# Decay rows of a chunked scan: repeated over the partitions by TensorE into PSUM instead of by a DRAM round trip

## The reference, cut to what matters

```python
cs = jnp.cumsum(dtc * a.reshape(G, R), axis=2)
seg = cs[:, :, :, None] - cs[:, :, None, :]
decay = jnp.where(tril, jnp.exp(jnp.where(tril, seg, 0.0)), 0.0)
cb = jnp.einsum('bcign,bcjgn->bcijg', cc, bc)
y_diag = jnp.einsum('bcijgr,bcjgrp->bcigrp', decay * cb[..., None], xdt)
...
y_off = jnp.einsum('bcign,bcgrpn,bcigr->bcigrp', cc, h_prev, jnp.exp(cs))
```

## Time and profile before

| what | value |
|---|---|
| median of three executions | 1598.22 us |
| the profiled execution | 1598.22 us |
| its span, first to last instruction | 1596.5 us |
| mean granted TensorE clock | 0.984 of full |
| busy share of the span: PE, DVE, ACT, POOL | 97%, 18%, 13%, 8% |
| mean DMA rate | 249 GB/s |

### The profile page before, as it was taken

How to read it: one execution, slowest core, us unless ns; L and a number is a source line. 1 busy time by engine, 2 the same in 40 slices (tenths; PEclk the granted TensorE clock), 3 DMA queues, 4 the chain that set the end, 5 groups by cost and what they waited for, 6 DMA issues and landing times.

```text
span 1596.5 us, 44448 instructions
## 1 busy us (share of the span) xinstructions
PE 1548.9 (97%) x20574; PEld 1305.1 (82%) x20574; DVE 284.1 (18%) x680; ACT 204.8 (13%) x527; POOL 131.4 (8%) x200
## 2 busy tenths in 40 slices
PE   7999999999999999998999999999999999999998
PEld 5667666666666667666999999999999999999897
DVE  2455520000000245553100000000000000000021
ACT  1245310000000034521000000000000000000000
POOL 4311125000000020111100000000000000000100
PEclk9999999999999999999899999999999999999999
DMA  9933429976323432332899999999999999999991
GB/s 250 269 114 89 128 82 273 334 246 218 119 93 113 112 112 67 100 117 93 280 355 343 358 359 352 357 346 339 369 349 355 356 346 359 344 365 360 348 354 36
DMA packets 199228, 397.39 MB, mean 249 GB/s; under 512 B 13723, under 2 KB 69667, under 8 KB 198889
## 3 DMA queue, kind: packets, MB, share of 16 engines
q1 hardware_dynamic: 180664, 346.26, 63.4%
q0 software_dynamic: 16816, 45.42, 9.4%
q10 hardware_dynamic: 1568, 2.91, 0.6%
HBM read 359.87 MB, written 36.63 MB: 248 GB/s over the span
## 4 chain that ended last, share of the span: by engine, by line
PE 95%; DVE 2%; issue 1%; ACT 1%; DMA 1%; SPq 0%; DVEq 0%; ACTq 0%
PE bank L1298 33%; PE bank L1320 16%; PE bank L1210 13%; PE bank L755 7%; PE bank L1227 6%; PE bank L1051 2%; PE bank L738 2%; PE bank L1068 2%; PE bank L724 1%; PE bank L1035 1%; PE bank L1024 1%; PE bank L1260 1%; PE bank L678 1%; PE bank L709 1%; PE bank L1041 1%
## 5 line engine op out<-in xcount | busy, mean ns | idle before, releaser
L1298 PE MATMUL bank<-arena,ring 128*64 128x108 f32 x11264 | 532.9, 257 | 9.6 <-issue 8.7
L1298 PEld LDWEIGHTS bank<-arena,ring 128*64 128x64 f32 x11264 | 526.8, 138 | 15.5 <-issue 13.1
L1320 PE MATMUL bank<-arena,ring 128*64 128x108 f32 x5632 | 263.2, 256 | 0.2
L1320 PEld LDWEIGHTS bank<-arena,ring 128*64 128x64 f32 x5632 | 261.7, 137 | 0.8 <-issue 0.6
L1210 PE MATMUL bank<-hnT,ring 128*128 128x336 f32 x704 | 200.8, 449 | 1.8 <-DVE hnT L1676 1.8
L1210 PEld LDWEIGHTS bank<-hnT,ring 128*128 128x128 f32 x704 | 134.6, 191 | 68.1 <-issue 3.2
L755 PE MATMUL bank<-hnT,ring 128*128 128x336 f32 x384 | 119.8, 457 | 0.0
L2133 DVE TENSOR_TENSOR arena<-arena,bank 128x432 f32<-128x432 f32 (+1 forms) x48 | 27.2, 567 | 509.3 <-PE bank L1298 509.3
L1227 PE MATMUL bank<-arena,ring 128*128 128x336 f32 x352 | 99.6, 446 | 0.0
L755 PEld LDWEIGHTS bank<-hnT,ring 128*128 128x128 f32 x384 | 70.5, 192 | 34.7 <-issue 6.4
L1227 PEld LDWEIGHTS bank<-arena,ring 128*128 128x128 f32 x352 | 66.9, 190 | 32.6
(11 more groups left out here) (360 smaller groups left out, 1079.1 us busy)
## 6 DMA issues: line engine op xcount, KB each, us to landing
ring<-in_moe_w_gate SPq DMA_DIRECT2D x88, 1024.0 KB, 6.2
ring<-in_moe_w_up SPq DMA_DIRECT2D x88, 1024.0 KB, 6.3
ring<-in_moe_w_down SPq DMA_DIRECT2D x88, 1024.0 KB, 5.9
ring<-in_w_in SPq DMA_DIRECT2D x16, 1024.0 KB, 6.7
ring<-in_w_gate SPq DMA_DIRECT2D x11, 1024.0 KB, 20.6
ring<-in_w_up SPq DMA_DIRECT2D x11, 1024.0 KB, 18.5
xg_rows<-arena POOLq DMA_DIRECT2D x1, 10800.0 KB, 71.8
y_rows<-arena POOLq DMA_DIRECT2D x1, 10800.0 KB, 112.8
```

The costliest lines, as they stand in the source:

```text
L1298: ins = mm(into[rows, SLOTS * fi:SLOTS * fi + SLOTS], weights[:, c, col:col + 64], xg[:, k0 + c, :], start=(k0 + c == 0 and fi == 0), stop ...
L1320: ins = mm(bank[5 + c // 4][rows, SLOTS * (c % 4):SLOTS * (c % 4) + SLOTS], weights[:, col:col + 64], hid[:, f, :], start=(f == 0 and c % ...
```

## The change

`csrow` no longer goes to DRAM. A new PE step `row_decays(pr)` multiplies, for each of the pair's two heads, a [8, 128] stationary tile (column h of the identity, repeated over 128 columns) with `csrow`, [8, 336]. The product puts the head's row on all 128 partitions of PSUM bank 3 or 4. ACT's `decays` reads that bank and waits for `seg_psum`. A bank is written again when `decay_exp` says that ACT has read it. `sample_states` uses bank 0 alone, and waits for DVE to have read its previous half. The stationary and moving operands need 8 partitions.

```diff
-        head_sums_kept = nc.dram_tensor("head_sums_kept", [LAYERS, HEADS, NT], F32, kind="Internal").ap()
...
-        decay = [take(544), take(512)] + [qk_[:, i * PCOLS:(i + 1) * PCOLS] for i in range(2)]
-        decay_rows = qk_[:, 2 * PCOLS:2 * PCOLS + 2 * NT]
+        decay = [take(544), take(512)] + [qk_[:, i * 512:(i + 1) * 512] for i in range(2)]
...
-        def sstate_bank(pr, q):
-
-            return 3 if q and pr < 3 else 0
...
+                def row_decays(pr):
+
+                    for h in (2 * pr, 2 * pr + 1):
+                        if h >= 2:
+                            pe.wait_ge(decay_exp, 8 * l + h - 1)
+                        mm(bank[3 + h % 2][:, 0:NT], ident[0:8, h:h + 1].to_broadcast([8, 128]), csrow, start=True, stop=True).then_inc(seg_psum, 1)
+
...
-                    if pr:
-                        pe.wait_ge(sstate_ready, 2 * n + (1 if pr == 3 and q else q - 1))
-                    mm(bank[sstate_bank(pr, q)][:, :], xw[pr % 2][0:80, 2, :], Bexp[0:80, 4 * q:4 * q + 4, :], start=True, stop=True).then_inc(sstate_psum, 1)
+                    if pr or q:
+                        pe.wait_ge(sstate_ready, 2 * n + q)
+                    mm(bank[0][:, :], xw[pr % 2][0:80, 2, :], Bexp[0:80, 4 * q:4 * q + 4, :], start=True, stop=True).then_inc(sstate_psum, 1)
...
                 sample_attend(1)
+                row_decays(0)
...
                 states_turned(0)
+                row_decays(1)
                 pe.wait_ge(mixsq_ready, 3 * l + 1)
...
                 for pr in range(4):
+                    if pr in (1, 2):
+                        row_decays(pr + 1)
                     if pr < 3:
                         states_turned(pr + 1)
...
                     if pr == 3:
+                        pe.wait_ge(decay_exp, 8 * (l + 1))
                         attention_part(4, 3)
...
-                def decay_rows_wanted(pr):
-                    act.wait_ge(sums_kept, 16 * (l + 1))
-                    if pr:
-                        act.wait_ge(decay_exp, 8 * l + 2 * pr)
-                    act.dma_start(decay_rows, head_sums_kept[l, 2 * pr:2 * pr + 2].rearrange("h t -> (h t)").partition_broadcast(128)).then_inc(decay_rows_here, 16)
-
...
-                        act.dma_start(head_sums_kept[l], csrow).then_inc(sums_kept, 16)
...
-                        R, E = decay_rows[:, NT * hh:NT * hh + NT], decay[h % 4]
-                        act.wait_ge(decay_rows_here, 16 * (4 * l + pr + 1))
+                        R, E = bank[3 + hh], decay[h % 4]
+                        act.wait_ge(seg_psum, 8 * l + h + 1)
...
-                    v.tensor_tensor(h0_[pr][:, 512 * q:512 * q + 512], h0_[pr][:, 512 * q:512 * q + 512], bank[sstate_bank(pr, q)][:, :], ALU.add).then_inc(sstate_ready, 1)
+                    v.tensor_tensor(h0_[pr][:, 512 * q:512 * q + 512], h0_[pr][:, 512 * q:512 * q + 512], bank[0][:, :], ALU.add).then_inc(sstate_ready, 1)
```

More of the change, by code:

```diff
@@ L405, in hymba_step @@
             sem(x) for x in ("s_probT_psum", "s_probT_dve", "s_probT_act", "s_att_psum"))
-        cb_psum, cb_ready, sums_kept, decay_rows_here, decay_exp, M_ready, ypair_psum, y_ready, Bexp_ready = (
-            sem(x) for x in ("cb_psum", "cb_ready", "sums_kept", "decay_rows_here", "decay_exp", "M_ready", "ypair_psum", "y_ready", "Bexp_ready"))
+        cb_psum, cb_ready, seg_psum, decay_exp, M_ready, ypair_psum, y_ready, Bexp_ready = (
+            sem(x) for x in ("cb_psum", "cb_ready", "seg_psum", "decay_exp", "M_ready", "ypair_psum", "y_ready", "Bexp_ready"))
         h0T_psum, h0T_act, h0T_dve, xw_ready, pstate_ready, sstate_psum, sstate_ready, half_psum, half_added = (
@@ L1541, in _ @@
                         act.wait_ge(tail_cols_ready, l + 1)
-                        decay_rows_wanted(0)
                     if u == 21:
@@ L1588, in _ @@
                 act.wait_ge(att_mixed, 3 * (l + 1))
-                decay_rows_wanted(1)
                 f(att_squares, mixT[:, 4:8, 256:NT], ACT.Square).then_inc(mixsq_ready, 1)
@@ L1596, in _ @@
                 states_turned(1)
-                decay_rows_wanted(2)
                 decays(2)
                 states_turned(2)
-                decay_rows_wanted(3)
                 decays(3)
```

## The result

The changed kernel took 1603.14 us (median of 16 runs, 1592.22 to 1610.46). The kernel before, on the same chip, took 1592.58 us (median of 16, 1588.70 to 1600.17). The ratio is 1.0054, with an interval of 1.0036 to 1.0073: the change costs 0.54%, some 8.6 us, and the interval leaves 5.7 to 11.6 us. Most of it is a fixed price of the new matmuls. The clock adds nothing that shows over many runs: the middle of their mean clocks is 0.984 for both kernels.

The account below looks back on a forecast made before the run. PE was taken as the bound: 3.89 us in layer 0 and 3.21 in layer 1 made 7.1, added to 1598.2, less 3.3 for a clock fall that goes, forecast 1602.0 us; the range ran from 1595.9 to 1608.6.

Parts of the forecast that it names:

- rival 4: ACT's DMA waits were on the path: all 11.3 us go, 9.04 come, 1595.9 us; chance 0.10.
- pairs 1 and 2: row_decays(2) and (3) at these pairs' starts, where PE runs without a break: nothing covers them, +2.26 us a layer.
- the passage: Serial stretch leading to layer 0's loop, with row_decays(0) ahead of the token rows: nothing covers its two matmuls, +1.13 us.
- pair 0: Layer 0, row_decays(1) ahead of L1116: partly hidden in PE's wait, 0.56 us of delay, taken as 0.5.
- so I keep 0.565: Price in us of one new matmul on PE, from 336-column float32 matmuls in the chain; two make a step of 1.13.
- Layer 1's passage and pair 0: row_decays(0) shifts DVE against POOL's L588, while PE's idle 2.10 us hides row_decays(1): middle of two cases, +0.95 us.
- DVE first: Layer 1: DVE's L1908 starts before POOL's L588, POOL is held 0.5 us, L1920 ends about 0.65 us later.
- POOL first: Layer 1: POOL's L588 starts before DVE's L1908, which is held instead of L1920; L1920 ends 1.2 us later.
- bound of 9.04 for all exposed: Upper end for both layers in us: four steps a layer at 1.13, 4.52 a layer, none hidden.
- -3.26: Layer 1's first fall of PE's clock, behind the idle time before pair 0's outputs, likelier than not goes: 3.26 us saved.
- Rival 3: New fall of the clock in layer 0's serial passage or at another PE wait in layer 1: 1608.6 us; chance 0.20.
- rival 5: Something else sets the time, as in the earlier run of 1590.5 us: at or under 1592; chance 0.05.

Follow-up runs that it names:

- two row tiles: Kernel before with a second tile for the rows, each pair's DMA asked for a pair earlier, no new matmul: 1590.30 us, ratio 0.9988.
- two filled kernels: Idle full-size matmuls in PE's waits: six a layer in the kernel before (1584.52 us, ratio 0.9946), five in the changed kernel (1597.29 us, 1.0020).
- before, once more: Kernel before, no edit, profiled a second time: one execution, 1598.96 us.
- placed one by one: Changed kernel with 128-partition row matmuls, several heads' matmuls placed apart, meant for where PE waits for DVE: 1591.95 us, ratio 0.9991.

## Why the prediction was right and wrong

**Right.** PE is the bound, and what the change adds is PE's time in the chain: the kernel before with the matmuls alone has the same loss. ACT's waits for the DMA were off the path (rival 4 falls with the two row tiles: 0.9988). ACT's new waits cost nothing; no L1036 was released by late decays, though ACT waited 32.5 us for PE. Right too was what lies bare: pairs 1 and 2 and the passage in full, pair 0 in part.

**The step that failed first: "nothing in the rows says that fewer partitions make a matmul shorter, so I keep 0.565".** I asked only whether a low tile would be quicker. It is dearer, by its neighbours: 1.46 us a step instead of 1.13. Term by term, forecast and measured at full clock: the passage of layer 0 1.13 and 1.32; pair 0 0.5 and 0.74; pairs 1 and 2 together 2.26 and 2.93. Layer 0: 3.89 forecast, 5.0 measured. A row that hints at it was in the trace of before, the 0.47 us ahead of the weight loads at 131.15, and I read PE's rows and not those of its loads; it shows that a change of height is paid, though not how much.

**Layer 1's passage and pair 0** had 0.95, between 0.65 (DVE first) and 1.2 (POOL first). Measured: +1.32 in the passage (the changed kernel's own has a fall of the clock in it, so this is from the same step in others: 6.79 us against 5.47), and pair 0 from 7.34 to 6.64, -0.70: +0.62 in all, as much as the end for DVE first. Layer 0's pair 0 took 5.90 us before, so the meeting of POOL and DVE cost layer 1 1.44; now pair 0 takes 6.64 in both layers, and PE no longer pays for it. But in the changed kernel's profile POOL and DVE hardly met. The timeline of DVE and POOL in the changed kernel, against the earlier trace rows:

```profile
674.72 1.89 POOL L582 TENSOR_TENSOR arena<-arena,const 80x1024 f32<-80x1024 f32 x1
...
676.47 0.56 DVE L1903 TENSOR_TENSOR arena<-arena,small 128x384 f32<-128x384 f32 x1
...
677.88 0.67 DVE L1915 TENSOR_TENSOR arena<-arena 128x496 f32<-128x496 f32 x1
```

POOL's L582 ends at 676.61, while L1903 (before: L1908) has just begun, and L1915 (before: L1920, 2.11 us) has its 0.67; the passage was late by its own fall of the clock. With 64 partitions and no such fall the same instructions meet:

```profile
669.08 2.55 POOL L582 TENSOR_TENSOR arena<-arena,const 80x1024 f32<-80x1024 f32 x1
669.32 0.55 DVE L1903 TENSOR_TENSOR arena<-arena,small 128x384 f32<-128x384 f32 x1
...
670.74 1.42 DVE L1915 TENSOR_TENSOR arena<-arena 128x496 f32<-128x496 f32 x1
```

POOL's takes 2.55 us instead of 1.89 and DVE's L1915 1.42 instead of 0.67: first POOL is held through L1903, then DVE through POOL's rest, and pair 0 takes 6.65 us all the same. That is the case of DVE first as forecast. It is the rule that the prediction quoted from the Trainium skill ("SBUF — State Buffer", "SBUF: two separate sides") in its other case, with one difference: POOL's record starts 0.24 us before DVE's, and it is POOL that is lengthened by about L1903's time. The start of a record doesn't say who holds the port. With pairs 1 and 2 (2.93) layer 1 is 3.6, forecast 3.21.

The sum: 8.6 us, forecast 7.1, measured 8.6 over the runs and 8.9 between the two filled kernels. That is within the forecast's own bound of 9.04 for all exposed, but for another reason: at 1.46 a step that bound is 11.7, and 3.1 of it don't show: 1.4 are hidden in PE's waits at pair 0, 0.3 are saved in the passages (1.32 a step and not 1.46), and 1.4 are what layer 1's meeting no longer costs. The match of 8.6 with 8.6 is better than it deserves: the interval is 3 us wide to either side, and what the experts give back isn't in the sum.

**The step that failed second: the clock's term as a whole, "-3.26".** The fall that it speaks of did go. From pair 0's outputs of layer 1 to the next `sample_states`, 4.75 us at full clock, all three profiled executions with neither new matmuls nor filling show a fall, and none of the seven with the new matmuls does. What failed is that its price was booked as the change of the clock over the whole kernel, as if no other fall came in its place. The table has the profiled executions, in us. Its first column of numbers is the way from `states_turned(0)` to pair 0's outputs, at full clock 5.90 before, 6.64 with low tiles and some 6.3 with full ones; the other three go from a pair's outputs to the next `sample_states`, at full clock 4.75.

| kernel | layer 0, up to pair 0 | layer 0, pair 3 | layer 1, pair 0 | layer 1, pair 3 |
|---|---|---|---|---|
| before | 5.90 | 4.76 | 8.01 | 6.37 |
| before, once more | 5.91 | 8.01 | 9.07 | 8.01 |
| two row tiles | 5.90 | 4.75 | 6.36 | 4.75 |
| changed | 8.26 | 8.01 | 4.75 | 8.01 |
| before with the matmuls | 8.28 | 8.01 | 4.75 | 4.75 |
| 32 partitions | 8.28 | 8.01 | 4.75 | 6.18 |
| 64 partitions | 6.64 | 4.75 | 4.76 | 6.19 |
| 128 partitions | 6.25 | 6.28 | 4.75 | 8.01 |
| placed one by one | 6.37 | 4.75 | 4.75 | 4.75 |

The falls in the scans cost 4.9 and 11.2 us in the two profiles of before and 9.4 in that of the changed kernel; over the runs the mean clocks are 0.984 in the middle for both (33 executions of each), and nothing in them asks for a term other than 0. Rival 3 had a part in it: in the profiled execution of after the clock fell in layer 0 at the end of the passage, where it looked for a fall, for 1.6 us, and at pair 3 at the price it had (3.25 us). Three of the four profiles with low tiles and no filling have that first fall and none of those of before does; whether the new matmuls bring it about isn't shown by so few. With PE's waits filled neither scan fell in any of the three profiles. Among the changed kernel's 33 executions the clock tells the fast from the slow: five with a mean clock of 0.989 or more have a median of 1594.1 us, the other 28 one of 1603.1.

**The chances.** The difference forecast was +3.8 us, inside the 0.5% (8.0 us) that counted as no change (0.67). Measured is +8.6, just beyond it (0.26), with an interval that reaches to both sides of the line, so it can't be told which of the two came to pass. With the clock left as it was and the step at its true price the same sum would have said +8.6. The range held the time, but on a base that was 5.6 us too high, and that is luck; three runs with two of them at 1598.3 and one at 1590.5 said that the base was uncertain, and I used this only for rival 5.

**Left open.** How much of the scans' time the experts give back wasn't measured. Which condition makes the clock fall at one wait and not at another, in the same program, wasn't tried further.

## What to carry to other kernels

A matmul that takes the place of a DMA wait is worth it only where that wait reaches the bound; take the wait away by itself first, as the two row tiles did. On PE, price a small matmul together with its neighbours: two matmuls whose tile has another height than its neighbours' cost 0.3 us more here than two filled up with zeros to 128 partitions, and one of these set into a wait of PE cost 0.1 us instead of 0.57. A clock term belongs in a prediction only as the difference between many executions, and a fall that goes at one place says little while others may come. Where PE waits, cheap idle matmuls may be worth more than the change that is being studied.

## What the hardware showed that I had not expected

- A float32 tile of 8, 32 or 64 partitions between tiles of 128: +1.46 to +1.47 us for two matmuls of 336 columns; with 128 partitions +1.17. The next load of a full tile stood idle for 0.47 us.
- Six idle matmuls a layer: 0.9946 of the time before; with seven more in the router 0.9919. The picking's 48 matmuls took 5.62 us instead of 10.59.
- Two executions of one program: layer 0's scan 56.38 and 59.63 us, layer 1's 62.69 and 65.75, by where the clock fell and for how long. The fall behind layer 1's pair 0 was in all three profiles without new or idle matmuls and in none of the seven with the new ones.
- A POOL instruction whose record starts first was held by the DVE instruction that starts 0.24 us later (2.55 us instead of 1.89), and then held the next one (1.42 instead of 0.67).
